# First block's merge: branch and output products as three float32r products of split halves, and two of three attention rounds for the large products

## The chip, the cores and the metric

The kernel runs on one core of one Trainium2 chip. The metric is the device time of one execution, in microseconds (us). TensorE (PE) multiplies, VectorE (DVE), ScalarE (ACT) and GpSimd (POOL) work on elements, SyncE (SP) issues the transfers from memory into a ring of five buffers in on-chip memory.

## What is computed

Two blocks on a sequence of 256 tokens with 1024 features, all in float32. The change is in the end of the first block. There two branches, `ya` (a gated delta rule) and `yb` (windowed attention with a sink, 8 heads of 64), are gated, projected, added and projected again:

```python
def _merge(ya, yb, ga, gb, w_proj_a, w_proj_b, w_out):
    y = jax.nn.sigmoid(ga) * (ya @ w_proj_a) + jax.nn.sigmoid(gb) * (yb @ w_proj_b)
    return y @ w_out

# in _layer: ga and gb are 1024-column slices of h @ w_in
ob = _latent_attention(qb, kb, vb, kb_c, vb_c, sink)
yb = ob * jax.nn.silu(zb)
x = x + gate[:, None] * _merge(ya, yb, ga, gb, w_proj_a, w_proj_b, w_out)
```

`ya`, `yb` are 256 x 512, `w_proj_a`, `w_proj_b` 512 x 1024, `w_out` 1024 x 1024. The second block (two layers, each with a feed-forward part, a mixer and a second feed-forward part) starts with a norm of the new `x` and takes the rest of the kernel.

## The kernel before

Every engine has a program of its own, written as a chain of Python functions. A step notes a name with `done(ins, name)`, a later step on any engine waits with `wait_ge(name)`. Each engine works strictly through its own list, so what stands ahead of a waiting instruction, and behind it, is set by the order in which the Python code is run. Where two or more things run beside each other on one engine, `run(...)` (L114) takes one step of each generator in turn: one such turn is called a round here. `slow(t, n)` (L125) gives a generator one step in every n rounds.

The stretch around the change has four parts.

1. **Attention** (`pe_attention` L1406, `act_attention` L1459, `v_attention` L1492). Four units u = 0 to 3, each 128 queries by 4 heads. For a unit PE makes four score products (into four PSUM banks), ACT copies their context half (L1473), DVE masks the other half (L1507), DVE takes the maximum (L1512) and some small steps (L1513 to L1515), ACT exponentiates (L1477, L1479), DVE finishes the denominator (L1517, L1518), PE transposes the probabilities (L384), ACT (L1485) and DVE (L1526) copy the transposes out, PE multiplies by the values (`ps<-arena ... 128x64`), DVE scales the result (L1530). The order on PE is: scores 0, scores 1, values 0, scores 2, values 1, scores 3, values 2, values 3; each is cut in halves of two heads. A unit's transposes wait for its softmax.
2. **Beside it** (`pe_beside` L1599 and its partners, slowed by n = 2): the last two column groups of `h @ w_in` (groups 5 and 6, the gate of branch b; on PE each is 16 products of 128x512, in four pieces of four), the norm and gate of `ya` (DVE L1631), its four transposes ("ya" turns), and the product with `w_proj_a` in four pieces of four matmuls (`ps<-ring,arena`), each multiplied into the gate by DVE (L1638). A third generator, `mods`, computes vector-matrix products for later gates, mostly on DVE (L522).
3. **Merge** (`pe_merge`, `act_merge`, `v_merge` L1642): DVE gates `yb` (L1645), PE transposes it (8 transposes), ACT copies the transposes out (L1561), PE multiplies by `w_proj_b` (16 matmuls of 128x512), DVE gates and adds (L1650, L1652, for each block of 128 tokens), PE transposes the sum (16), ACT copies (L1561), PE multiplies by `w_out` (32 matmuls of 128x512).
4. **Join**: DVE adds to `x` (L1734, L1740), ACT, DVE and POOL make the norm, PE transposes, and the first feed-forward part starts.

The matmuls of the merge are float32: each is written as two records in the trace. The feed-forward parts already work in another way: a float32 matrix is split into a high half, rounded to float32r (ACT L1913 for weights), and a low half, the difference (DVE L1962), and `mm3` (L386) makes three products, high x high, high x low, low x high, each one record.

SP's list holds, in this order, the loads of groups 5 and 6, of `w_proj_a` (2 MB in two buffers), `w_proj_b` (two), `w_out` (four) and the first feed-forward weights. A load waits until the buffer five loads earlier is released.

## Time and profile before

| | us |
|---|---|
| median of 3 runs | 1693.09 (1693.08 to 1705.6) |
| the profiled execution's own time | 1702.35 |
| its span, first to last instruction | 1700.6 |
| attention with what runs beside it, 307.8 to 414.6 | 106.8 |
| merge, 414.6 to 468.0 | 53.4 |
| all the rest | 1540.4 |

The profile is one execution. PE is busy for 92% of its span; busy does not mean full speed, since the profile also gives the clock that PE was granted (1.00 is 2.4 GHz, 0.50 is 1.2 GHz), and a matmul's record is longer than the distance to the next. DVE is busy for 60%, ACT 39%, POOL 14%.

### The profile page before, as it was taken

The numbers are of one execution on the slowest core, as the hardware profiler recorded it, in microseconds if no ns is written. First come the engines' busy times: TensorE is split into PE (matmuls) and PEld (weight loads), VectorE is DVE, ScalarE is ACT, GpSimd is POOL, SyncE is SP. The second block draws the span as 40 slices with busy tenths as digits, with TensorE's granted clock in tenths as the row PEclk, the third lists the DMA queues.
The fourth block names the chain that finished last, engine by engine and source line by source line (L and its number), as shares of the span: only waits on it lengthen the run. The fifth ranks groups of instructions, "written<-read, shape, count | busy, mean of one in ns | idle before, by whom it ended". The sixth has DMA issues, their size and how long they took to land.

```text
span 1700.6 us, 19133 instructions
## 1 busy us (share of the span) xinstructions
PE 1563.1 (92%) x7536; PEld 1154.5 (68%) x7536; DVE 1018.4 (60%) x1518; ACT 667.0 (39%) x1082; POOL 233.5 (14%) x243
## 2 busy tenths in 40 slices
PE   7997999888979989999979999799988999989998
PEld 1646566445468877775558877688877865477886
DVE  0477685741178887355348886478886453376654
ACT  2425221331155543361235552455532531155642
POOL 0231172000001100042001110011100241011100
PEclk9998999997989999999989998999999999989999
DMA  9434233531348879332347787378976322457551
GB/s 343 148 126 148 88 118 118 162 122 50 112 161 282 288 267 335 96 106 81 118 134 254 253 286 269 115 247 259 314 288 215 124 74 99 136 172 230 193 198 50
DMA packets 192096, 305.27 MB, mean 180 GB/s; under 512 B 6139, under 2 KB 116487, under 8 KB 191879
## 3 DMA queue, kind: packets, MB, share of 16 engines
q1 hardware_dynamic: 189088, 299.45, 52.3%
q10 hardware_dynamic: 2919, 4.61, 0.7%
q8 instruction: 59, 0.97, 0.2%
q14 instruction: 30, 0.25, 0.0%
HBM read 302.99 MB, written 1.05 MB: 179 GB/s over the span
## 4 chain that ended last, share of the span: by engine, by line
PE 69%; DVE 15%; ACT 7%; issue 3%; DMA 3%; POOL 2%; ACTq 0%; DVEq 0%; SPq 0%; POOLq 0%
PE ps L381 67%; DVE accs L522 3%; DVE wlo L1962 2%; DMA ring<-in_ffn_w_down_dram 2%; ACT whi L1913 2%; PE ps L384 1%; DVE H L1985 1%; DMA ring<-in_w_mod_dram 1%; ACT arena L1479 1%; DVE arena L1218 1%; DVE arena L1215 1%; DVE H L1800 1%; DVE misc L1512 1%; DVE H L1734 1%; ACT hh L1918 0%
## 5 line engine op out<-in xcount | busy, mean ns | idle before, releaser
L381 PE MATMUL ps<-hh,whi 128*128 128x512 f32 x1408 | 496.6, 404 | 27.1 <-DVE hh L1968 21.6
L1962 DVE TENSOR_TENSOR wlo<-ring,whi 128x1024 fp32r<-128x1024 f32 x264 | 323.8, 1231 | 180.9 <-ACT whi L1913 172.6
L1913 ACT ACTIVATE whi<-ring 128x1024 fp32r<-128x1024 f32 x264 | 273.4, 1054 | 280.1 <-PE ps L381 240.4
L381 PE MATMUL ps<-hh,wlo 128*128 128x256 f32 x1408 | 373.1, 286 | 0.0
L381 PEld LDWEIGHTS ps<-hh,whi 128*128 128x128 f32 x1408 | 259.2, 192 | 81.3 <-DVE hh L1968 22.4
L381 PE MATMUL ps<-ring,H 128*128 128x512 f32 (+1 forms) x608 | 268.7, 595 | 16.4 <-ACT arena L1013 9.0
L381 PEld LDWEIGHTS ps<-hh,wlo 128*128 128x128 f32 x1408 | 271.3, 193 | 17.1 <-issue 1.7
L381 PEld LDWEIGHTS ps<-ring,H 128*128 128x128 f32 x608 | 116.1, 197 | 141.9 <-issue 121.4
L522 DVE SCALAR_TENSOR_TENSOR accs<-ring,misc,accs 128x512 f32<-128x512 f32 x266 | 204.8, 770 | 2.6
L381 PE MATMUL ps<-H,ring 128*128 128x256 f32 (+1 forms) x576 | 157.5, 432 | 1.8 <-DVE H L1800 0.8
L381 PE MATMUL ps<-whi,ahi 128*128 128x512 f32 x352 | 143.2, 407 | 9.0 <-DVE H L1985 9.0
L381 PEld LDWEIGHTS ps<-arena 128*128 128x128 f32 (+3 forms) x1320 | 124.2, 171 | 33.5 <-issue 18.0
L381 PE MATMUL ps<-arena 128*128 128x64 f32 (+6 forms) x1320 | 136.8, 266 | 10.5 <-DVE arena L1526 6.8
L381 PEld LDWEIGHTS ps<-H,ring 128*128 128x128 f32 x576 | 109.8, 192 | 46.2 <-issue 30.6
L381 PE MATMUL ps<-wlo,ahi 128*128 128x512 f32 x352 | 139.9, 397 | 0.0
L381 PE MATMUL ps<-whi,alo 128*128 128x512 f32 x352 | 139.6, 397 | 0.0
L1951 POOL TENSOR_TENSOR alo<-H,ahi 128x256 fp32r<-128x256 f32 x88 | 66.7, 758 | 521.7 <-ACT ahi L1943 518.2
L381 PE MATMUL ps<-ring,arena 128*128 128x512 f32 x192 | 89.5, 623 | 3.3 <-ACT arena L2112 2.7
L381 PEld LDWEIGHTS ps<-whi,ahi 128*128 128x128 f32 x352 | 67.9, 193 | 25.3 <-DVE H L1985 10.3
L381 PEld LDWEIGHTS ps<-wlo,ahi 128*128 128x128 f32 x352 | 67.9, 193 | 14.9 <-issue 1.2
L381 PEld LDWEIGHTS ps<-whi,alo 128*128 128x128 f32 x352 | 67.8, 193 | 14.6
L1936 ACT ACTIVATE H<-ps 128x512 f32<-128x512 f32 x88 | 52.7, 599 | 58.0 <-PE ps L381 58.0
(290 smaller groups left out, 1410.5 us busy)
## 6 DMA issues: line engine op xcount, KB each, us to landing
ring<-in_w_mod_dram SPq DMA_DIRECT2D x84, 1024.0 KB, 7.3
ring<-in_w_in_dram SPq DMA_DIRECT2D x48, 1024.0 KB, 5.1
ring<-in_ffn_w_gate_dram SPq DMA_DIRECT2D x44, 1024.0 KB, 5.7
ring<-in_ffn_w_up_dram SPq DMA_DIRECT2D x44, 1024.0 KB, 5.7
ring<-in_ffn_w_down_dram SPq DMA_DIRECT2D x44, 1024.0 KB, 6.1
ring<-in_w_out_dram SPq DMA_DIRECT2D x12, 1024.0 KB, 4.8
gates<-in_b_mod_dram SPq DMA_DIRECT2D x7, 512.0 KB, 6.4
ring<-in_w_proj_a_dram SPq DMA_DIRECT2D x2, 1024.0 KB, 5.0
```

The costliest lines, as they stand in the source:

```text
L381: return self.e.matmul(o, lhsT, rhs, start=start, stop=stop)
L384: return self.e.transpose(o, in_, self.M.C["ident"])
L522: v.op(v.e.scalar_tensor_tensor(a, src, w, a, ALU.mult, ALU.add), *keys, *([("mod sum", c.n)] if kt == 7 else []))
L1215: v.op(v.e.tensor_tensor(t, M.AT[:, k, 0:k].unsqueeze(2).broadcast_to([128, k, w_]), M.XS[:, k, k:32].unsqueeze(1).broadcast_to([128, k, w ...
L1218: v.op(v.e.tensor_tensor(x, x, t, ALU.add))
L1479: a.done(a.e.activation(sm[:, t4, :], sm[:, t4, :], ACT.Exp, bias=nm[:, t4:t4 + 1], accum_out=den[:, t4:t4 + 1]), ("soft", u))
L1512: v.op(v.e.tensor_reduce(mx, sm, AX.X, ALU.max))
L1734: v.done(v.e.scalar_tensor_tensor(res[hf], two(M.ps((*ps, blk, hf))), factor, two(M.gates[:, gi, cols[hf]]), ALU.mult, ALU.mult), ("gated" ...
L1913: a.done(a.e.activation(hi, M.slot(key)[:, r0:r0 + rn, :], ACT.Copy), ("whi", l, sub, n))
L1936: a.done(a.e.activation(SG[x % 3], M.psum[:, b:b + 2, 256:512], ACT.Copy), ("copied", l, sub, x))
L1951: g.op(g.e.tensor_tensor(M.ALO[:, f, :], SG[f % 3][:, 0, :], plain(M.AHI[:, f, :]), ALU.subtract), ("alo", l, sub, f))
L1962: v.done(v.e.tensor_tensor(lo, M.slot(key)[:, r0:r0 + rn, :], plain(hi), ALU.subtract), ("split", l, sub, n), *([M.freed(key)] if ends els ...
```

## The change

The products with `w_proj_b` and `w_out` become three float32r products each, as in the feed-forward parts. The weights of `w_proj_b` are split into a high half by ACT, in the attention's last rounds (`act_beside`), and a low half by POOL, which is written back into the ring buffer (`ring_r` is the ring seen as float32r). For `w_out` ACT makes the high halves of the eight row groups (six once the attention is over, two after the second transposes), POOL the low halves of the first four, DVE of the other four. The transposed `yb` and sum are split too: ACT writes the high half where it wrote the copy before, DVE the low half. The products no longer wait for all transposes but for each one's low half. `slow` now gives the work beside the attention two steps in three rounds. ACT waits for the end of the `w_out` product before it writes the first feed-forward weights, because a high half lies there.

```diff
-def slow(t, n):
-    for _ in t:
-        for _ in range(n):
+def slow(t):
+    for i, _ in enumerate(t):
+        for _ in range(1 + i % 2):
             yield
...
+        self.HB = [self.WLO[:, 2, :], self.WLO[:, 3, :], alo[:, 2560:3584], alo[:, 3584:4608]]
+        self.HM = [k4(ahi, 0), k4(ahi, 1), self.WHI[:, 1, :], self.WLO[:, 0, :], k4(ahi, 2), k4(ahi, 3), self.WHI[:, 0, :], self.WHI[:, 3, :]]
...
 def pool_attention(g):
     pool_rstd(g, "o", 8)
+    for name in ("b", "m"):
+        for kt in range(4):
+            low_rows(g, name, kt)
...
+def pe_out(pe, name, lhs, nk):
+    M, (lhi, llo) = pe.M, lhs
...
+        key, _, hi, lo = merge_weights(M, name, kt)
+        pe.wait_ge(("rows split", name, kt), ("turned low", {"b": "yb", "m": "mt"}[name], kt))
+        c = slice(blk * 128, (blk + 1) * 128)
+        for hf in range(2):
+            s = slice(hf * 512, hf * 512 + 512)
+            ins = pe.mm3(bs[blk][hf], (lhi[:, kt, c], llo[:, kt, c]), (hi[:, s], lo[:, s]), kt == 0, kt == nk - 1)
...
-            ins = pe.mm(bs[blk][hf], lhs[:, kt, blk * 128:(blk + 1) * 128], M.slot(key)[:, kt % 2, hf * 512:hf * 512 + 512],
-                        kt == 0, kt == nk - 1)
...
+def act_high_rows(a, name, kt, *after):
+    key, w, hi, _ = merge_weights(a.M, name, kt)
+    a.wait_ge(key, *after)
+    a.done(a.e.activation(hi, w, ACT.Copy), ("rows high", name, kt))
...
+def low_rows(lane, name, kt):
+    _, w, hi, lo = merge_weights(lane.M, name, kt)
+    lane.wait_ge(("rows high", name, kt))
+    lane.done(lane.e.tensor_tensor(lo, w, plain(hi), ALU.subtract), ("rows split", name, kt))
...
+        v.done(v.e.tensor_tensor(lo[:, k, :], M.ps(key)[:, 0:256], plain(hi[:, k, :]), ALU.subtract), ("free", key), ("turned low", name, k))
...
 def act_beside(a):
...
     yield from act_turn(a, "ya", M.YAT, 2, 4, ("yat",))
+    for kt in range(4):
+        yield
+        act_high_rows(a, "b", kt)
...
 def act_merge(a):
     M = a.M
-    run(act_turn(a, "yb", M.YBT, 2, 4, ("ybt",)))
-    run(act_turn(a, "mt", M.MT, 2, 8, ("mt",)))
+    act_turn_high(a, "yb", M.YBH, 4)
+    for kt in range(6):
+        act_high_rows(a, "m", kt, ("o", "a", 1, 1), ("pv", 3, 3))
+    act_turn_high(a, "mt", M.MTH, 8)
+    for kt in (6, 7):
+        act_high_rows(a, "m", kt)
```

The order of instructions shows where the work beside the attention now stands. First PE, in the middle of the attention. In these rows `ring,H` is a piece of four products of column groups 5 and 6, `arena 128x512` are scores, `ctab,arena` are transposes (8 are half a unit's, 2 one "ya" turn), `arena 128x64` are products with the values, and `accs,ctab` belongs to `mods`. Before, from the second piece of group 6 to the values of unit 1:

```order
L381 MATMUL ps<-ring,H 128x512 x4
L381 MATMUL ps<-arena 128x512 x2
L381 MATMUL ps<-accs,ctab 128x512
L381 MATMUL ps<-arena 128x512 x2
L381 MATMUL ps<-ring,H 128x512 x4
L384 MATMUL ps<-ctab,arena 128x128 x8
L381 MATMUL ps<-ring,H 128x512 x4
L384 MATMUL ps<-ctab,arena 128x128 x8
L381 MATMUL ps<-arena 128x64 x8
```

and with the change, from the third piece of group 6 to the same values:

```order
L398 MATMUL ps<-ring,H 128x512 x4
L398 MATMUL ps<-arena 128x64 x8
L398 MATMUL ps<-ring,H 128x512 x4
L398 MATMUL ps<-arena 128x512 x2
L398 MATMUL ps<-accs,ctab 128x512
L398 MATMUL ps<-arena 128x512 x2
L401 MATMUL ps<-ctab,arena 128x128 x22
L398 MATMUL ps<-arena 128x64 x8
```

Both large pieces that stood behind the scores of unit 2 are ahead of them now; behind them stand 22 transposes alone (unit 1's 16 and three "ya" turns).

Second PE from the scores of unit 3 to the transposes of `yb` (the last 8). `ring,arena` is a piece of the product with `w_proj_a`. Before:

```order
L381 MATMUL ps<-arena 128x512 x2
L384 MATMUL ps<-ctab,arena 128x128 x20
L381 MATMUL ps<-arena 128x64 x16
L381 MATMUL ps<-ring,arena 128x512 x4
L384 MATMUL ps<-ctab,arena 128x128 x16
L381 MATMUL ps<-ring,arena 128x512 x4
L381 MATMUL ps<-arena 128x64 x16
L381 MATMUL ps<-ring,arena 128x512 x8
L384 MATMUL ps<-ctab,arena 128x128 x8
```

and with the change:

```order
L398 MATMUL ps<-ring,arena 128x512 x4
L398 MATMUL ps<-arena 128x512 x2
L398 MATMUL ps<-ring,arena 128x512 x4
L401 MATMUL ps<-ctab,arena 128x128 x8
L398 MATMUL ps<-ring,arena 128x512 x4
L401 MATMUL ps<-ctab,arena 128x128 x8
L398 MATMUL ps<-ring,arena 128x512 x4
L398 MATMUL ps<-arena 128x64 x16
L401 MATMUL ps<-ctab,arena 128x128 x16
L398 MATMUL ps<-arena 128x64 x16
L401 MATMUL ps<-ctab,arena 128x128 x8
```

The four pieces moved from behind unit 3's scores to among them and unit 2's transposes, and nothing large is left between the end of the attention and the transposes of `yb`.

Third ACT, from the scores of unit 3 to the last high half of `w_out`, with the change (`wlo<-ring`, `alo<-ring` up to the four copies of `yb`'s transposes, `wlo<-ps`, are the high halves of `w_proj_b`):

```order
L1493 ACTIVATE arena<-ps 128x256 x4
L1614 ACTIVATE wlo<-ring 128x1024
L1497 ACTIVATE misc<-misc 128x4
L1499 ACTIVATE arena,misc<-arena,misc 128x512 x4
L1505 ACTIVATE arena<-ps 128x512
L1614 ACTIVATE wlo<-ring 128x1024
L1505 ACTIVATE arena<-ps 128x512
L1614 ACTIVATE alo<-ring 128x1024 x2
L1505 ACTIVATE arena<-ps 128x512 x2
L1637 ACTIVATE wlo<-ps 128x256 x4
L1614 ACTIVATE ahi<-ring 128x1024 x2
L1614 ACTIVATE whi<-ring 128x1024
```

Before, the rows with `ring` were not there.

## Rows read from the trace of the kernel before

**Rows 1.** The page: engines, busy us, share of the span, instructions.
```profile
span 1700.6 us, 19133 instructions
PE 1563.1 (92%) x7536; PEld 1154.5 (68%) x7536; DVE 1018.4 (60%) x1518; ACT 667.0 (39%) x1082; POOL 233.5 (14%) x243
```

**Rows 2.** Stretches: length, busy us of each engine, PE clock, transfers.
```profile
core 0: us, PE busy (x) PEld busy (x) DVE busy (x) ACT busy (x) POOL busy (x), PEclk, DMA share, GB/s
372.10:414.60 42.50, 34.65 (x143) 22.61 (x143) 13.15 (x23) 8.90 (x21) 0.00 (x0) 0.84 0.07 25
```

**Rows 3.** PE in order of time, attention: start, us, what; idle before, its releaser.
```profile
331.81 1.91 PE L384 MATMUL ps<-ctab,arena 128*128 128x128 f32 x16
338.64 6.34 PE L381 MATMUL ps<-ring,H 128*128 128x512 f32 x8 [4.92 <-ACT arena L1013]
344.82 3.68 PE L381 MATMUL ps<-arena 128*128 128x64 f32 x32
...
356.79 3.70 PE L381 MATMUL ps<-ring,H 128*128 128x512 f32 x8
...
366.62 2.00 PE L381 MATMUL ps<-arena 128*128 128x64 f32 x16 [0.94 <-DVE arena L1526]
...
370.29 3.81 PE L381 MATMUL ps<-arena 128*128 128x64 f32 x20
...
376.30 2.40 PE L384 MATMUL ps<-ctab,arena 128*128 128x128 f32 x20
384.56 7.09 PE L381 MATMUL ps<-arena 128*128 128x64 f32 x32 [5.85 <-DVE arena L1526]
391.44 5.53 PE L381 MATMUL ps<-ring,arena 128*128 128x512 f32 x8
...
398.56 3.60 PE L381 MATMUL ps<-ring,arena 128*128 128x512 f32 x8
```

**Rows 4.** DVE in order of time: unit 3's maximum, the rest of its softmax.
```profile
377.36 2.29 DVE L1512 TENSOR_REDUCE misc<-arena 128x4 f32<-128x2048 f32 x1
...
383.40 0.16 DVE L1517 TENSOR_TENSOR misc<-misc 128x4 f32<-128x4 f32 x1 [3.16 <-ACT arena L1479]
```

**Rows 5.** PE in order of time, the merge.
```profile
414.60 1.06 PE L384 MATMUL ps<-ctab,arena 128*128 128x128 f32 x8 [2.01 <-DVE arena L1645]
416.31 17.07 PE L381 MATMUL ps<-ring,arena 128*128 128x512 f32 x32 [0.65 <-ACT arena L1561]
436.11 3.60 PE L384 MATMUL ps<-ctab,arena 128*128 128x128 f32 x16 [2.73 <-DVE arena L1652]
440.19 27.73 PE L381 MATMUL ps<-ring,H 128*128 128x512 f32 x64 [0.47 <-ACT H L1561]
```

**Rows 6.** PE in order of time, a feed-forward part's split products, 27 records.
```profile
655.05 0.39 PE L381 MATMUL ps<-whi,ahi 128*128 128x512 f32 x1
...
660.94 0.39 PE L381 MATMUL ps<-whi,alo 128*128 128x512 f32 x1
```

**Rows 7.** Groups of instructions: count, busy us, mean ns, idle before.
```profile
L381 PEld LDWEIGHTS ps<-wlo,ahi 128*128 128x128 f32 x34 | 6.4, 188 | 1.3
L1913 ACT ACTIVATE whi<-ring 128x1024 fp32r<-128x1024 f32 x264 | 273.4, 1054 | 280.1 <-PE ps L381 240.4 <-DMA ring<-in_ffn_w_down_dram 35.2 <-DMA ring<-in_ffn_w_up_dram 4.2
L2322 POOL TENSOR_TENSOR arena<-arena 128x1024 f32<-128x1024 f32 x12 | 25.2, 2102 | 68.8 <-DVE arena L2264 63.6 <-DVE arena L2277 4.9
L1951 POOL TENSOR_TENSOR alo<-H,ahi 128x256 fp32r<-128x256 f32 x88 | 66.7, 758 | 521.7 <-ACT ahi L1943 518.2
L1561 ACT ACTIVATE arena<-ps 128x256 f32<-128x256 f32 x8 | 2.7, 382 | 16.6 <-PE ps L384 16.6
L1990 DVE TENSOR_TENSOR H<-H 128x256 f32<-128x256 f32 x88 | 37.0, 422 | 7.2 <-ACT H L1939 1.8
L1740 DVE TENSOR_TENSOR X<-X,H 128x512 f32<-128x512 f32 x28 | 18.5, 683 | 0.0
L2274 DVE TENSOR_TENSOR arena<-arena 128x512 f32<-128x512 f32 x16 | 16.4, 1026 | 41.7 <-ACT arena L2223 23.7 <-PE ps L381 13.3 <-ACT arena L2224 4.2
```

**Rows 8.** ACT in order of time: the first feed-forward weights' high half.
```profile
476.67 1.06 ACT L1913 ACTIVATE whi<-ring 128x1024 fp32r<-128x1024 f32 x1
```

More of the change, by code:

```diff
@@ L205, in sb, with twice @@
         return self.ctx.enter_context(self.nc.sbuf_tensor(name, shape, f32))
+    def twice(self, name, shape):
+        with self.nc.sbuf_tensor(name, shape, f32) as plain_:
+            pass
+        return plain_, self.sbr(f"{name}_r", shape)
     def sbr(self, name, shape):
@@ L1562, in act_turn @@
         yield
+def pe_out(pe, name, lhs, nk):
+    M, (lhi, llo) = pe.M, lhs
+    bs = [[pe.bank(("o", name, blk, hf), "outx") for hf in range(2)] for blk in range(2)]
+    for blk, kt in [(b_, k_) for k_ in range(nk - 4) for b_ in range(2)] + [(b_, k_) for b_ in range(2) for k_ in range(nk - 4, nk)]:
+        key, _, hi, lo = merge_weights(M, name, kt)
[4 more added lines that the diff above has]
+            ins = pe.mm3(bs[blk][hf], (lhi[:, kt, c], llo[:, kt, c]), (hi[:, s], lo[:, s]), kt == 0, kt == nk - 1)
+        if kt == nk - 1 or (blk and kt % 2):
+            pe.done(ins, *([("o", name, blk)] if kt == nk - 1 else []), *([M.freed(key)] if blk else []))
 def sp_out(sp, name, w, nk):
@@ L1567, in sp_out, with merge_weights, v_turn, act_turn_high @@
         sp.full_rows(("out", name, k0), w, k0, 2)
-def pe_out(pe, name, lhs, nk):
-    M = pe.M
-    bs = [[pe.bank(("o", name, blk, hf), "outx") for hf in range(2)] for blk in range(2)]
-    for blk, kt in [(b_, k_) for k_ in range(nk - 4) for b_ in range(2)] + [(b_, k_) for b_ in range(2) for k_ in range(nk - 4, nk)]:
-        key = ("out", name, kt // 2 * 2)
-        pe.wait_ge(key)
-        for hf in range(2):
-            ins = pe.mm(bs[blk][hf], lhs[:, kt, blk * 128:(blk + 1) * 128], M.slot(key)[:, kt % 2, hf * 512:hf * 512 + 512],
-                        kt == 0, kt == nk - 1)
-        if kt == nk - 1 or (blk and kt % 2):
-            pe.done(ins, *([("o", name, blk)] if kt == nk - 1 else []), *([M.freed(key)] if blk else []))
+def merge_weights(M, name, kt):
+    key = ("out", name, kt // 2 * 2)
+    return key, M.slot(key)[:, kt % 2, :], (M.HB if name == "b" else M.HM)[kt], M.slot_r(key)[:, kt % 2, :]
+def act_high_rows(a, name, kt, *after):
[6 more added lines that the diff above has]
+    lane.done(lane.e.tensor_tensor(lo, w, plain(hi), ALU.subtract), ("rows split", name, kt))
+def v_turn(v, name, hi, lo, nk):
+    M = v.M
+    for k in range(nk):
+        key = ("turn", name, k)
+        v.wait_ge(("turned high", name, k))
+        v.done(v.e.tensor_tensor(lo[:, k, :], M.ps(key)[:, 0:256], plain(hi[:, k, :]), ALU.subtract), ("free", key), ("turned low", name, k))
+def act_turn_high(a, name, hi, nk):
+    M = a.M
+    for k in range(nk):
+        key = ("turn", name, k)
+        a.wait_ge(key)
+        a.done(a.e.activation(hi[:, k, :], M.ps(key)[:, 0:256], ACT.Copy), ("turned high", name, k))
 def sp_beside(sp):
@@ L1593, in sp_merge @@
     I = sp.M.I
-    run(slow(sp_beside(sp), 2), mods)
+    run(slow(sp_beside(sp)), mods)
     sp_out(sp, "b", I["w_proj_b"][0], 4)
@@ L1645, in v_merge @@
     v.done(v.e.tensor_tensor(M.OB, M.OB, M.ZB, ALU.mult), ("yb gated",))
+    v_turn(v, "yb", M.YBH, M.YBL, 4)
+    for kt in (4, 5):
+        low_rows(v, "m", kt)
     for blk in range(2):
@@ L2666, in tensor_program @@
     pe.sums = "row"
-    run(pe_attention(pe), slow(pe_beside(pe), 2), mods)
+    run(pe_attention(pe), slow(pe_beside(pe)), mods)
     pe.sums = "mods"
@@ L2688, in vector_program @@
     v.fence("delta")
-    run(v_attention(v), slow(v_beside(v), 2), mods)
+    run(v_attention(v), slow(v_beside(v)), mods)
     v_merge(v)
```

24 lines of the change are left out of this document (17 added, 7 removed).

## The prediction

> **What bounds the kernel now.** I read the page first: PE is busy for 92% of 1700.6 us [rows 1], so a change counts by what it does to PE's list, in matmul time, idle time and clock. Then the stretches: from the scores of unit 3 (372.1) to the transposes of `yb` (414.6) PE is busy for 34.65 of 42.5 us at a clock of 0.84 [rows 2]. Then PE in order of time, which shows where idle time and low clock lie. In the attention PE stands for 4.92 us until ACT has copied group 5 out (338.64), and for 5.85 us until DVE has copied unit 2's transposes (384.56). After each stop the clock is at its lower level: eight records of 128x512 take 6.34 and then 5.53 us, where they take 3.60 at the upper one, and 32 value records take 7.09 instead of 3.68 [rows 3]. So the first stop costs 4.92 + 2.7, the second 5.85 + 3.4 + 1.9. In the merge the reader sees a product of 17.07 us and one of 27.73 us, with only short stops around them [rows 5]: there matmul time is the price.
>
> **The two products.** A float32 matmul of 128x512 is two records; 64 take 27.73 us [rows 5], 0.867 us for a matmul. Three split products stand 0.2265 us apart (26 distances from 655.05 to 660.94 [rows 6]), 0.680 us. That saves 0.187 us each: 32 in the `w_out` product, **6.0 us** (27.7 to 21.8), and 16 in the `w_proj_b` product, **3.0 us**. The latter took 17.07 us, 3.2 more than 32 records at the upper clock (13.87); I keep these 3.2, since PE comes from the same kind of stop (2.01 us, eight transposes, 0.65 us).
> The Trainium skill (FP8 and Floating Point Precision, TensorE Precision Notes) says that true FP32 takes four passes through the array. With three single passes in their place a quarter would go, 3.5 and 6.9 us, 10.4 in all where the rows give 9.0; the rows' distance is 0.2265 us, and I go by it.
>
> **Starts of the products.** Before, the first matmul waited for all transposes to be copied, now only for its own row's high and low half. For `yb`: 1.71 us lay from the first transpose to the product (414.60 to 416.31 [rows 5]); now about 0.45 to the first transpose's end and its latency, 0.38 ACT, 0.42 DVE (the kind of [rows 7]): 1.3. For the sum: PE stands 0.47 us [rows 5] until the last copy, now nothing, as the first rows are split while PE transposes the others. **0.4 us** each.
>
> **The splits.** High halves: twelve on ACT at 1.054 us. Low halves: eight on POOL, four on DVE. The nearest rows for a POOL one are 2.10 us (128x1024, float32) and 758 ns for a quarter of it to float32r, so 3.03 at most [rows 7]; I take 2.1 to 3.0. ACT makes the first high half of `w_proj_b` before unit 3's softmax, the other three by 22 us after unit 3's scores begin; POOL is done with all at 28 to 31, and the product starts at 32.4. Hidden. For `w_out` ACT works from 33.0 to 39.3, POOL from 34 to 43 or 46, and the product starts at about 53. DVE's two (2.5 us) fall under the `w_proj_b` product, the last two of ACT and DVE under the first ten of sixteen pieces of the `w_out` product. Without that cover the first would cost ACT 1.05 + POOL 2.1 to 3.0. ACT's new wait ahead of the first feed-forward weights costs nothing: it came to them 8.7 us after the end of the `w_out` product (476.67 [rows 8] against 467.92 [rows 5]). Behind it stand only its own later splits. SP's list is the same; buffers come free earlier.
>
> **The attention.** PE has the same work, in another order.
> Up to 331.8 PE never stops, and the same ten pieces come first, so nothing changes. Then group 6 needs group 5 copied out; with that copy now ahead of unit 1's softmax on ACT, PE goes on at about 332.0: the stop of 4.92 and its 2.7 of low clock go. From there: first piece 3.6, transposes 1.9, piece 3.5, wait for DVE's copy 0.9 (its softmax 1 ends at 340.4), values 3.7, two pieces 7.2, scores and `mods` sum 4.9: the scores of unit 2 end at about 357.7. Before they ended at 356.79 with two pieces less done [rows 3].
> But these two pieces were what covered unit 2's softmax. From the end of the scores to the next values it takes 9.8 us (356.79 to 366.62 [rows 3]). PE now has 3.2 us of transposes for it, so **a new stop of some 6.4 us** opens, to 367.5. As the stops of 4.92 and 5.85 us lowered the clock and cost 2.7 and 5.3 us by that, I take 3.8 here. With 5.3 us of work (values 3.8, a "ya" turn, a sum) unit 3's scores begin at 376.6 instead of 372.1 (370.29 plus 16 of 20 records [rows 3]).
> From there on, t in us after that start: scores 1.9, piece 3.5, scores 1.9, piece 3.5, to 10.8. DVE multiplies that piece (0.7) before it takes the maximum, so the softmax starts at 11.5 and ends at 18.0 (2.29 + 0.65 + ACT 3.0 + 0.5; before 377.36 to 383.8 [rows 4]). PE in the meantime: transposes and pieces to 19.8, unit 2's values to 23.5, unit 3's transposes 25.4, values 29.2, then DVE's scaling and gating, 0.42 and 1.22 with gaps: transposes of `yb` at 31.1. Before that took 42.5 [rows 2]. The stop of 5.85 us and its low clock are gone here, and so are 8 us that the pieces took after it.
> Start of the transposes: 376.6 + 31.1 = 407.7 instead of 414.6, **6.9 us**. Bounds: if no clock loss belonged to short stops, before and after, the gain is 2.7 (403.9 against 406.6); if the new stop did not open, 10.6.
>
> **Sum.** 6.9 + 0.4 + 3.0 + 0.4 + 6.0 = 16.7 us. All behind the merge moves with it. The profiled execution's own time, 1702.35, would become 1685.7. It is 9.3 us above the median of the runs, 1693.09, so the median should be **1676.4 us**.
>
> **Rivals.**
> 1. The attention gains nothing (17 in 100). The new stop is as long as both old ones, or the clock stays low through the pieces behind it (7 us more for four at half speed). For it: the stop is 0.5 us longer than the longest before. Against it: unit 3 is shorter by 11.4. Only 9.8 us are left: 1683.3.
> 2. POOL and DVE hold each other up (12 in 100). For it: DVE's 128x512 with both inputs in `arena`, in a stage where POOL works too, takes 1026 ns where 683 is usual [rows 7]. A merge addition (L1652) or a split behind a POOL operation would wait 2.1 to 3.0 us; on the path is the second block's addition, and POOL should be done by then. Gain 13.7, time 1679.4. It turns into a PE wait if one POOL low half takes over 4.8 us (19 us for four).
> The Trainium skill (SBUF — State Buffer, Who interferes with whom) states that a DVE instruction with two SBUF inputs and a GpSimd instruction that reads SBUF shut each other out for the whole instruction. By it the DVE low halves of `w_out`, both inputs in SBUF, wait for POOL, while those of the transposes, one input from PSUM, do not.
> 3. The new stop hardly opens, as softmax 2 starts earlier than I work out (8 in 100): gain up to 20.4, 1672.7.
> 4. Slower (3 in 100): the weight load of a product is not hidden, when the moving half lies in the ring and the stationary one in `alo`. It takes 188 ns [rows 7] against a distance of 226; put end to end 414 ns, 144 times: 59.8 us instead of 32.6, a loss of 18 against float32's 41.6, and with the attention's 6.9 and the starts' 0.8 the kernel is 10 us slower, 1703.6. It decides from a distance of 0.343 us on (0.2265 + 16.7 / 144). The feed-forward rows speak against it.
> The forecast has 60 in 100.
>
> **Numbers.** A difference under 1% is about what a measurement of this kernel can't tell from none; 1% is 1676.2. The forecast's own range is 1672 to 1681, so it lies on both sides of the line: a little over half of its 60 and all of case 3 make 0.43 for faster; the rest of it and cases 1 and 2 make 0.53 for the same; 0.04 slower. The range takes in cases 1 to 3 and the bounds of the attention with the lower price of the products (2.7 + 9.0: 1681; 10.6 + 11.2: 1671) and some for runs whose clock falls otherwise: 1668 to 1687.
>
> **What would show it.** Right: `w_out`'s 96 records in about 22 us, `w_proj_b`'s 48 in 11 to 14.5; no stop for ACT L1030 at 332; one of 5 to 7 us ahead of unit 1's values; none of over 1.5 us from unit 3's scores to its end; PE in the merge released by DVE's low halves (L1629), never by POOL's (L1620). Wrong: a PE wait for L1620 (case 2), two stops of 5 us in the attention (case 1), split products over 0.25 us apart at the upper clock (case 4), or the gain given back in the feed-forward part behind.

## The result and the profile after

In paired runs the changed kernel takes 1680.96 us (median of six, 1680.03 to 1683.97), the kernel before 1699.13 us (median of six, 1693.08 to 1705.6). The ratio is 0.9895, with a 95% interval from 0.9875 to 0.9916: a gain of 1%, with the interval wholly below 1. A kernel counts as faster here only from 2% on, so the changed one is "the same", and so it is for every kernel below, down to the best ratio of 0.9828. The prediction drew the line at 1%, and its 0.43 for "faster" against 0.53 for "the same" was split at that line. The profiled execution took 1683.97 us (before 1702.35), its span is 1682.2 us (before 1700.6).

The page's head, as [rows 1] for before:
```profile
span 1682.2 us, 19265 instructions
PE 1550.8 (92%) x7584; PEld 1162.7 (69%) x7584; DVE 1031.2 (61%) x1534; ACT 678.1 (40%) x1094; POOL 254.3 (15%) x251
```
PE is busy for 12 us less; DVE, ACT and POOL have the splits on top.

PE of the changed kernel in order of time (start, us, what; idle before and its releaser), to compare with [rows 3] and [rows 5]:
```profile
341.83 2.01 PE L398 MATMUL ps<-arena 128*128 128x64 f32 x16 [1.01 <-DVE arena L1546]
343.67 5.35 PE L398 MATMUL ps<-ring,H 128*128 128x512 f32 x8
...
368.88 3.68 PE L398 MATMUL ps<-arena 128*128 128x64 f32 x16 [7.21 <-DVE arena L1546]
...
406.71 1.06 PE L401 MATMUL ps<-ctab,arena 128*128 128x128 f32 x8 [1.87 <-DVE arena L1704]
409.04 0.80 PE L398 MATMUL ps<-wlo 128*128 128x512 f32 x1 [1.27 <-DVE whi L1629]
409.64 0.63 PE L398 MATMUL ps<-ring_r,wlo 128*128 128x512 f32 x1
410.06 0.63 PE L398 MATMUL ps<-wlo,whi 128*128 128x512 f32 x1
...
413.02 0.40 PE L398 MATMUL ps<-wlo,whi 128*128 128x512 f32 x1
...
421.38 0.40 PE L398 MATMUL ps<-alo,whi 128*128 128x512 f32 x1
424.50 2.61 PE L401 MATMUL ps<-ctab,arena 128*128 128x128 f32 x16 [2.73 <-DVE arena L1714]
428.17 0.80 PE L398 MATMUL ps<-ahi,alo 128*128 128x512 f32 x1 [1.06 <-DVE alo L1629]
...
466.09 0.79 PE L398 MATMUL ps<-hh,whi 128*128 128x512 f32 x1 [5.11 <-DVE hh L2039]
```
The reader is to see four things: one stop of 7.21 us in place of two of 4.92 and 5.85; a product that begins behind a wait for DVE's low halves (L1629); matmuls 0.43 us apart at a product's start and 0.232 later; and the first feed-forward matmul at 466.09, where it was at 481.71. So 15.6 of the 18.4 us come from the code that was changed. The distance of 0.43 us for 512 columns belongs to the 1.2 GHz level, 0.232 to 2.4: from 429 to 433 us, where most of the matmuls stand 0.43 apart, the granted clock is 0.57, from 433 to 452, where they stand 0.232 apart, 1.00.

### The profile page after: what moved, and what is told of

It reads as the page before. It is cut to its first block, busy times and chain, and to the rows that moved or that the text cites. A ratio compares the mean times of both kernels' runs of the same rounds, so it can differ in the third digit from the quotient of the medians.

```text
span 1682.2 us, 19265 instructions
## 1 busy us (share of the span) xinstructions
PE 1550.8 (92%) x7584; PEld 1162.7 (69%) x7584; DVE 1031.2 (61%) x1534; ACT 678.1 (40%) x1094; POOL 254.3 (15%) x251
## 4 chain that ended last, share of the span: by engine, by line
PE 70%; DVE 14%; ACT 7%; issue 3%; DMA 3%; POOL 2%; ACTq 0%; DVEq 0%; SPq 0%; POOLq 0%
PE ps L398 69%; DVE accs L539 3%; DVE wlo L2033 2%; ACT whi L1982 1%; DMA ring<-in_ffn_w_down_dram 1%; PE ps L401 1%; DVE H L2056 1%; DMA ring<-in_w_mod_dram 1%; DVE arena L1235 1%; DVE arena L1232 1%; DVE H L1803 1%; DVE H L1869 0%; ACT hh L1987 0%; DMA ctab<-in_consts_dram 0%; ACT H L1878 0%
## 5 line engine op out<-in xcount | busy, mean ns | idle before, releaser
L2033 DVE TENSOR_TENSOR wlo<-ring,whi 128x1024 fp32r<-128x1024 f32 x264 | 323.5, 1230 | 178.0 <-ACT whi L1982 170.4
L398 PEld LDWEIGHTS ps<-hh,wlo 128*128 128x128 f32 x1408 | 271.2, 193 | 16.7 <-issue 1.4
L398 PE MATMUL ps<-ring,H 128*128 128x512 f32 (+1 forms) x544 | 239.8, 593 | 11.0 <-ACT arena L2183 5.6
L398 PEld LDWEIGHTS ps<-ring,H 128*128 128x128 f32 x544 | 103.8, 198 | 120.2 <-issue 104.9
L398 PE MATMUL ps<-whi,alo 128*128 128x512 f32 x376 | 148.4, 398 | 0.0
L398 PEld LDWEIGHTS ps<-whi,alo 128*128 128x128 f32 x376 | 72.5, 193 | 15.8
L398 PE MATMUL ps<-ring,arena 128*128 128x512 f32 x160 | 70.8, 595 | 2.6 <-ACT arena L2183 2.6
```

What stands on the lines that cost most here:

```text
L398: return self.e.matmul(o, lhsT, rhs, start=start, stop=stop)
L2033: v.done(v.e.tensor_tensor(lo, M.slot(key)[:, r0:r0 + rn, :], plain(hi), ALU.subtract), ("split", l, sub, n), *([M.freed(key)] if ends els ...
```

## Experiments: the two parts, each alone

**The order alone.** The kernel before with the new pattern of steps:
```
-def slow(t, n):
-    for _ in t:
-        for _ in range(n):
+def slow(t):
+    for i, _ in enumerate(t):
+        for _ in range(1 + i % 2):
             yield
```
(and the calls without the 2).

> The kernel before with one edit, the work beside the attention at two steps in three rounds; float32 products as before. Theory A (the order of the attention is worth its own 7 to 8 us, whatever the products are): 7 to 9 us faster than the kernel before, the transposes of yb near 406.7, a stop of about 7 us before unit 1's values, w_out's 64 records again in about 27.7 us. Rival B (the gain comes from the split products, and the order only moves a stop from one unit to another): within 2 us of the kernel before.

**The products alone.** The changed kernel with every second step again:
```
-        for _ in range(1 + i % 2):
+        for _ in range(2):
```


> The changed kernel with the work beside the attention back at every second round; the split products stay. Theory A: 7 to 10 us faster than the kernel before, 8 to 10 slower than the changed one, the transposes of yb near 414 to 416 and the stop of 5.85 us before unit 2's values back; the high halves of w_proj_b come partly after the attention now (ACT takes steps 14 to 17 of its list in rounds 27 to 33), so POOL's low halves of 2.35 us each may make PE wait 1 to 5 us at the w_proj_b product. Rival B: as fast as the changed kernel to 2 us.

Measured: the order alone 1687.78 us, ratio 0.9939 (0.9917 to 0.9961); the products alone 1685.45 us, ratio 0.9932 (0.9908 to 0.9955). PE with the order alone, and then with the products alone:
```profile
369.19 3.67 PE L381 MATMUL ps<-arena 128*128 128x64 f32 x16 [7.21 <-DVE arena L1526]
407.08 1.06 PE L384 MATMUL ps<-ctab,arena 128*128 128x128 f32 x8 [1.87 <-DVE arena L1645]
408.80 15.70 PE L381 MATMUL ps<-ring,arena 128*128 128x512 f32 x32 [0.65 <-ACT arena L1561]
427.22 1.94 PE L384 MATMUL ps<-ctab,arena 128*128 128x128 f32 x16 [2.73 <-DVE arena L1652]
430.03 27.73 PE L381 MATMUL ps<-ring,H 128*128 128x512 f32 x64 [0.88 <-ACT H L1561]
```
```profile
338.15 6.26 PE L398 MATMUL ps<-ring,H 128*128 128x512 f32 x8 [4.93 <-ACT arena L1030]
384.01 7.09 PE L398 MATMUL ps<-arena 128*128 128x64 f32 x32 [5.85 <-DVE arena L1546]
436.66 0.50 PE L398 MATMUL ps<-ahi,alo 128*128 128x512 f32 x1 [1.73 <-DVE alo L1629]
472.48 0.79 PE L398 MATMUL ps<-hh,whi 128*128 128x512 f32 x1 [5.05 <-DVE hh L2039]
```
The attention's gain belongs to the order: with it alone the `yb` transposes come at 407.08, 7.5 us earlier, and with the products alone both old stops are back. The `w_out` product took 27.73 us with the order alone; with the products alone it ran from 436.66 to 459.1, 22.4 us. The first feed-forward matmul comes 10.1 and 9.2 us earlier, with both parts 15.6: they don't add up, since the lower clock falls at other places in each (below).

For the order alone, theory A holds: transposes, stop and `w_out` product are as expected, and the time is 11.1 us under that of the kernel before (7 to 9 expected). For the products alone the rows are those of theory A, the old stops and the transposes at 414.00, but its times are not: 13.5 us faster than the kernel before, where 7 to 10 were expected, and 4.5 slower than the changed one, where 8 to 10 were. The trace has 6.4 us between the two up to the first feed-forward matmul. The wait for POOL did not come: PE waits 1.27 us at the `w_proj_b` product, for DVE (L1629), as in the changed kernel.

## Experiments: what stands before the products

**Other banks.** In the changed kernel the `yb` transposes use banks 7, 0, 1, 2 and the product behind them starts in bank 2. Its first matmul therefore waits for the last transpose's low half, though its own operands are there. The eight `mt` transposes end in bank 2 too.
```
+ "yb": (7, 6, 4, 5), "mt": (2, 3, 0, 1, 4, 5, 6, 7)}
-    run(pe_turn(pe, "yb", M.OB, 2, 4, "all", ("yb gated",)))
+    run(pe_turn(pe, "yb", M.OB, 2, 4, "yb", ("yb gated",)))
-    run(pe_turn(pe, "mt", M.GA, 2, 8, "all", ("merged",)))
+    run(pe_turn(pe, "mt", M.GA, 2, 8, "mt", ("merged",)))
```


> The changed kernel with other PSUM banks for the transposes of yb (7, 6, 4, 5) and of the sum (2, 3, 0, 1 first). In the changed kernel the first bank of each product (2) is the one that the last transpose holds, so PE waits 1.27 and 1.06 us until DVE has made all low halves. Theory A (it is the bank, not the first row's low half): the two stops shrink to 0.3 us and nothing, 1 to 2 us faster than the changed kernel. Rival B (the stop is ACT's and DVE's latency for the first row): stops and time unchanged. Rival C: stops shrink, but the clock is at its lower level for as long, so that less than 1 us is gained.

Measured: 1676.49 us, ratio 0.9862 (0.9837 to 0.9887). PE:
```profile
407.53 1.06 PE L401 MATMUL ps<-ctab,arena 128*128 128x128 f32 x8 [1.87 <-DVE arena L1704]
408.96 0.47 PE L398 MATMUL ps<-wlo 128*128 128x512 f32 x1 [0.37 <-DVE whi L1629]
425.32 2.51 PE L401 MATMUL ps<-ctab,arena 128*128 128x128 f32 x16 [3.42 <-DVE arena L1714]
427.86 0.76 PE L398 MATMUL ps<-ahi,alo 128*128 128x512 f32 x1
```
The bank was the cause: 1.43 us from the start of the transposes to the product instead of 2.33, and 2.54 instead of 3.67. But 0.7 us of it goes back at once, in a stop of 3.42 instead of 2.73 before the `mt` transposes. That is DVE, late for the gating, as the next experiments show. From the `yb` transposes to the first feed-forward matmul the path is 1.7 us shorter (57.67 us instead of 59.38). The runs can't tell that much: the intervals of both kernels overlap.

**POOL works longer.** Rows 4 and 5 of `w_out` are split by POOL, behind its other eight, instead of DVE:
```
-    for name in ("b", "m"):
-        for kt in range(4):
+    for name, nk in (("b", 4), ("m", 6)):
+        for kt in range(nk):
             low_rows(g, name, kt)
```


> The changed kernel with the low halves of w_out's rows 4 and 5 taken from DVE and given to POOL, behind its other eight. Nothing is left out. Theory (POOL and DVE hold each other up when both read SBUF, and it costs nothing in the changed kernel only because the last addition of the gating, 1.22 us, falls just behind POOL's end): POOL now works on until about 426 us, that addition takes 2.1 to 2.7 us, the mt transposes begin 0.9 to 1.5 us later (at 425.4 to 426.0 in place of 424.50) and the time grows by that, 0.1%. Rival (there is no such contention, DVE's 2.7 us had another cause): the addition stays at 1.22, the transposes at 424.5, and the time is the same.

Measured: 1679.61 us, ratio 0.9898 (0.9874 to 0.9922), the same as the changed kernel within the interval, which is wider than what was to be seen. The trace decides. DVE and POOL of the changed kernel first, then DVE, POOL and PE of this one:
```profile
413.12 5.43 DVE L1620 TENSOR_TENSOR ring_r<-ring,ahi 128x1024 fp32r<-128x1024 f32 x2 [4.13 <-ACT ahi L1614]
418.47 1.27 DVE L1712 TENSOR_TENSOR arena<-arena,ps 128x512 f32<-128x512 f32 x2
419.78 2.12 DVE L1714 TENSOR_TENSOR arena<-arena 128x1024 f32<-128x1024 f32 x1
423.13 1.22 DVE L1714 TENSOR_TENSOR arena<-arena 128x1024 f32<-128x1024 f32 x1
...
417.43 3.38 POOL L1620 TENSOR_TENSOR ring_r<-ring,wlo 128x1024 fp32r<-128x1024 f32 x1
```
```profile
423.87 2.40 DVE L1712 TENSOR_TENSOR arena<-arena 128x1024 f32<-128x1024 f32 x1
...
417.13 2.44 POOL L1620 TENSOR_TENSOR ring_r<-ring,wlo 128x1024 fp32r<-128x1024 f32 x1
419.48 5.70 POOL L1620 TENSOR_TENSOR ring_r<-ring,ahi 128x1024 fp32r<-128x1024 f32 x2
...
426.41 3.60 PE L401 MATMUL ps<-ctab,arena 128*128 128x128 f32 x16 [3.90 <-DVE arena L1712]
```
The last addition, 1.22 us when POOL has finished, takes 2.40 beside it, and PE's stop is 3.90 instead of 2.73. (The path up to the first feed-forward matmul is no longer for it, 59.29 us from the `yb` transposes instead of 59.38: in this execution the `w_out` product ran at the upper clock from its start.) DVE's low halves of the rows take 2.7 us each beside POOL, as against 1.23 (1230 ns, the mean of 264 such subtractions in the feed-forward parts), and POOL's 3.38 us instead of 2.4. So rival 2's mechanism is in the changed kernel; it costs nothing there, but only just. DVE is busy without a pause from 413.12 to 421.90, and the product that it waits for ends at about 421.8; the next operation of DVE, which needs that product, begins at 421.82. The Trainium skill (SBUF — State Buffer, Who interferes with whom) says that a DVE instruction with two SBUF inputs and a GpSimd instruction that reads SBUF exclude each other; the rows agree. L1712 has one input from PSUM and was not stretched: two take 1.27 us at 418.47, beside POOL's subtraction, and 1.28 us with the order alone, where POOL does nothing then.

## Experiments: the low clock

**Idle work in the merge's stops.** PE multiplies a piece of the identity, into a bank that is written anew later, while it would stand:
```
+def fill(pe, b, n):
+    if b in pe.held:
+        pe.wait_ge(("free", pe.held[b]))
+    for _ in range(n):
+        pe.mm(pe.M.psum[:, b, 0:64], pe.M.C["ident"], pe.M.C["ident"][:, 0:64])
+    fill(pe, 4, 15)
     run(pe_turn(pe, "yb", M.OB, 2, 4, "all", ("yb gated",)))
+    fill(pe, 4, 10)
     pe_out(pe, "b", (M.YBH, M.YBL), 4)
...
```
and the like, 22 ahead of the `mt` transposes and 8 ahead of the `w_out` product.

> The changed kernel with idle work on PE in its four stops of the merge: 15, 10, 22 and 8 small products (128x64, of the identity, into a bank that is written anew later) ahead of the yb transposes, w_proj_b's product, the mt transposes and w_out's product. Nothing of the reference is left out. Theory (the low clock in the two products follows the stops): no distance of 0.43 us is left between the products' matmuls, w_proj_b's product takes 48 x 0.2325 = 11.2 us in place of 12.57 and w_out's 96 x 0.2325 = 22.3 in place of 24.53, the stops being no longer than they were; the first ffn matmul comes at 466.1 - 3.6 = 462.5 us, and the time is some 3.6 us under the changed kernel's (about 1677). Rival (the low clock has nothing to do with stops of 1 to 3 us, or the idle products run over into the transposes and take back what they give): the products keep 12.6 and 24.5 us, or a stop grows by what they save, and the first ffn matmul stays at 466 to 467.5.

The same with 7, 5, 11 and 4:

> The changed kernel with idle work on PE in the four stops of the merge again, at half the length (7, 5, 11 and 4 small products, 0.234 us each by the run with the long fill, so 1.6, 1.2, 2.6 and 0.9 us), so that it ends about when the stop does. Nothing is left out. Theory (the products ran slow at their start because PE had stood; the long fill cured it and lost the gain by running 1.1 to 2.3 us past each stop): the granted clock is 1.00 from 404 to 453 us, the stops end where they ended in the changed kernel, and the first ffn matmul comes 1.4 + 2.2 us before 466.09, at 462.5; median about 1677. Rival (short fills leave the clock low as the stops did): the products take 12.6 and 24.5 us and the first ffn matmul stays at 466.

Measured: the long fill 1677.15 us, ratio 0.9887 (0.9856 to 0.9917); the short one 1680.02 us, ratio 0.9899 (0.9884 to 0.9915). Stretches (length, busy us of each engine, granted clock) of the changed kernel, then with the long fill:
```profile
409.00:422.00 13.00, 12.74 (x48) 9.95 (x48) 8.85 (x6) 5.03 (x6) 11.43 (x4) 0.89 0.13 40
422.00:428.00 6.00, 2.61 (x16) 2.23 (x16) 4.96 (x11) 3.00 (x9) 0.00 (x0) 0.80 0.75 266
428.00:453.00 25.00, 24.52 (x96) 19.46 (x96) 5.24 (x8) 2.76 (x6) 0.00 (x0) 0.91 0.35 104
```
```profile
409.00:422.00 13.00, 13.00 (x67) 10.89 (x66) 8.83 (x9) 6.11 (x8) 11.48 (x4) 1.00 0.12 27
422.00:428.00 6.00, 6.00 (x55) 5.96 (x55) 3.67 (x5) 0.65 (x3) 0.00 (x0) 1.00 0.80 294
428.00:453.00 25.00, 25.00 (x120) 20.36 (x118) 7.35 (x14) 4.89 (x13) 0.00 (x0) 1.00 0.32 102
```
Without stops the clock is 1.00 throughout, and the two products take 11.2 and 22.3 us instead of 12.6 and 24.5. The long fill ran past the stops and took the gain back: the first feed-forward matmul came at 467.10, not at the 462.5 of the expectation. The median of 1677.15 that the expectation had named is not that gain, then; it came out by luck, in the rest of the program (1209.0 us in this profile, 1216.1 in the changed kernel's). The short one didn't, yet from the attention's last values (401.16 in the changed kernel, 396.15 here) to the first feed-forward matmul (466.09, 459.72) it needs 63.57 us instead of 64.93: 1.4 us gained, not the 3.6 of my expectation. (All of this execution lies 5 us earlier, since its clock was higher in code that is the same in both.) PE with the short fill:
```profile
415.24 2.56 PE L398 MATMUL ps<-ctab 128*128 128x64 f32 x22
419.47 1.94 PE L401 MATMUL ps<-ctab,arena 128*128 128x128 f32 x16 [1.67 <-DVE arena L1722]
423.13 0.50 PE L398 MATMUL ps<-ahi,alo 128*128 128x512 f32 x1 [0.88 <-DVE alo L1637]
```
From the product's end (415.24) to the `mt` transposes there are now 4.23 us instead of 2.89. The product ends 1.4 us earlier, DVE does not (5.42 us for its two low halves beside POOL): the margin is gone, and rival 2's price, 1.3 us, stands on the path. Another 0.6 us went in the join, where the lower clock fell on the first transposes (0.57 in their first microsecond instead of 0.92) and ACT got them 3.7 us after they began instead of 3.1.

**DVE's two low halves moved**, from ahead of the gating to behind the low halves of the `mt` transposes, in the kernel that has the other banks and the placement of the steps that is shown below:
```
-    for kt in (4, 5):
-        low_rows(v, "m", kt)
     ...
     v_turn(v, "mt", M.MTH, M.MTL, 8)
-    for kt in (6, 7):
+    for kt in (4, 5, 6, 7):
```


> Banks and placement as before, with DVE's low halves of w_out's rows 4 and 5 moved from ahead of the gating to behind the low halves of the mt transposes. Nothing is left out. Theory (once the product begins earlier, DVE is late to the gating since its low half beside POOL's takes 3.41 us, so rival 2's cost has come onto the path): the stop ahead of the mt transposes shrinks from 4.08 to about 2.7 us, w_out's product finds its rows 4 and 5 ready some 10 us after its start as before, and the first ffn matmul comes about 1.3 us earlier, near 460 us. Rival (the gating was bound by something else, or w_out's product now waits for row 4): the stop stays near 4 us, or a new stop stands in w_out's product and the first ffn matmul stays at 461.2 or later.

Measured: 1670.66 us, ratio 0.9843 (0.9827 to 0.9859). The stop before the transposes is 2.73 us where it was 4.08 with banks and placement together (first measured below), and no new one stands in the `w_out` product. The first half of the expectation holds; the second doesn't: the first feed-forward matmul came at 461.17, as before the move (461.20). The lower clock had fallen on the start of the `w_out` product (23.2 us instead of 22.3) and on the transposes of the join (13.9 us from the product's end to the first feed-forward matmul instead of 12.9).

## Experiments: another placement in the attention

The large products are placed by a table of steps, so that two of them stand beside unit 2's softmax:
```
+PE_AT = [1, 2, 4, 5, 7, 8, 13, 15, 18, 19, 20, 20, 21, 22, 23, 25]
-    run(pe_attention(pe), slow(pe_beside(pe)), mods)
+    run(pe_attention(pe), placed(pe_beside(pe), PE_AT), mods)
```
(and the like for DVE and ACT).

> The changed kernel with the steps beside the attention placed by a list of rounds: group 6's last two pieces behind unit 2's scores, three pieces of the w_proj_a product behind unit 3's, one ahead of unit 3's transposes. Theory A (the attention is bound by the softmax chain of 9.8 us per unit only where PE has no large piece to put behind the scores): the stop of 7.21 us before unit 1's values falls to under 1.5 us, its low clock (2.6 us) goes too, no stop over 1.5 us opens elsewhere, 6 to 9 us faster than the changed kernel. Rival B (the chain on DVE and ACT is as long as PE's work, so a stop only moves): a stop of 4 us or more opens at unit 2's or unit 3's values, less than 3 us faster.

Together with the other banks:

> The two single changes together that were each better than the changed kernel: other banks for the yb and mt transposes, and the large products placed at other steps of the attention. Nothing is left out. Theory (they work at different places, so they add up): yb transposes at 405.5, w_proj_b's product 1.4 us behind them, w_out's product without a stop, first ffn matmul at about 463.5, median 1667 to 1670. Rival (what the second gained was the low clock falling elsewhere by chance): the first ffn matmul is at 463.5 all the same, but the rest of the program takes 1210 to 1218 us in place of 1206 and the median is 1672 to 1677.

The latter with idle work ahead of the two rows of transposes and of the `w_proj_b` product:

> The kernel before this one (banks and placement) with idle work on PE ahead of the yb transposes (15 small products), of w_proj_b's product (3) and of the mt transposes (26). Nothing is left out. Theory (low clock follows the stops): both products run at 0.2325 us apart from their first matmul on, 11.2 and 22.3 us, the first ffn matmul comes 3 us earlier than without the fill (about 460.5), median some 3 us lower. Rival: no change of the products' times, first ffn matmul within 0.5 us of the kernel without the fill.

Measured: placement alone 1671.42 us, ratio 0.9841 (0.9817 to 0.9865); with the banks 1677.46, 0.9874 (0.9847 to 0.9901); with the fill 1679.91, 0.9902 (0.9879 to 0.9925). PE of the first:
```profile
345.01 7.39 PE L408 MATMUL ps<-arena 128*128 128x64 f32 x20 [0.52 <-DVE arena L1556]
...
358.05 5.37 PE L408 MATMUL ps<-ring,H 128*128 128x512 f32 x8
...
405.45 1.60 PE L411 MATMUL ps<-ctab,arena 128*128 128x128 f32 x8 [1.87 <-DVE arena L1714]
```
The stop of 7.21 us is gone, but the transposes come only 1.3 us earlier: behind two stops of 1.03 and 0.52 us PE ran at the lower clock from 345 to 361 us (20 records of 128x64 in 7.39 us, which take 3.8 at the upper level). The first feed-forward matmul comes at 464.39, 1.7 us earlier. The stop of 4 us or more that rival B expected elsewhere did not open, but its gain of less than 3 us is what the rows show. The runs show more: all four took 1669.53 to 1673.65 us, and the changed kernel's six 1680.03 to 1683.97. Of the 11.8 us between the two profiles 10.1 lie behind the first feed-forward matmul, in instructions that are the same. So theory A's 6 to 9 us came out in the time, but not from the attention; whether the placement has a part in them is not shown.

Banks and placement together bring the first feed-forward matmul to 461.20, the earliest until then, and the whole kernel is no faster for it. Here the expected median failed, and its rival, in the rest of the program, is what was seen (1214.4 us instead of 1206.0, median 1677.46). The fill, again at the long size, ran past the stops: the `w_proj_b` product began at 408.78 instead of 406.31, and the first feed-forward matmul came at 464.90.

**Does filling take the low clock away, or only move it?** In the kernel with rows 4 and 5 late: idle work in unit 0's stops, and ahead of both rows of transposes; then in unit 1's stops and ahead of the `w_proj_a` product too, of which this is the last form:
```
+            if u < 2 and t4 % 2 == 0:
+                for _ in range(4 - t4):
+                    pe.mm(bo[:, 256:320], M.C["ident"], M.C["ident"][:, 0:64])
...
+            if u == 1 and t4 == 1:
+                for _ in range(3):
...
+            for _ in range(0 if blk or hf else 2):
...
```


> The kernel with rows 4 and 5 late, with idle work on PE in the stop ahead of unit 0's values (4 small products), in the one inside them (2), ahead of the yb transposes (7) and of the mt transposes (11). Nothing is left out. Theory (the 17 us at the lower clock from 344 to 361 us come from the stops of 1.0 and 0.5 us there): PE runs at the upper clock there, which gives 8 us: yb transposes at 397 to 398 in place of 404.9, both products at 0.2325 us a matmul, first ffn matmul at 449 to 450, and the whole 6 to 10 us faster than the kernel without the fill. Rival (that stretch is not due to the short stops but to what PE did before, or is only put off): the lower clock stands there all the same or falls on later work, yb transposes at 403 or later, and the whole is within 3 us of the kernel without the fill.

> The kernel with rows 4 and 5 late and idle work in unit 0's stops, with idle work in the stops of unit 1 and ahead of w_proj_a's product too (4, 3, 2 and 2 small products), where the lower clock began in the run before (364 to 385 us, behind stops of 0.95, 0.73 and 0.52 us). Nothing is left out. Theory (the lower clock needs a stop of some tenths of a microsecond ahead of it, wherever it falls): with no stop over 0.4 us left between 340 and 404 us, the granted clock is 1.00 there, yb transposes come at 398 to 399 in place of 407.7, the first ffn matmul at 452 to 453, and the time is some 5 us under that of the kernel without this fill. Rival (the chip lowers the clock after so much work at the upper one, stops or not, so that filling only moves it): the low stretch stands there without a stop ahead of it, or comes later, yb transposes at 405 to 408 or the products slow, and the first ffn matmul stays at 460 to 462.

Measured: 1667.26 us, ratio 0.9833 (0.9809 to 0.9857), and 1668.42 us, ratio 0.9828 (0.9808 to 0.9848). Stretches of both:
```profile
340.00:362.00 22.00, 20.80 (x103) 13.05 (x101) 15.26 (x27) 7.92 (x18) 0.00 (x0) 1.00 0.34 123
362.00:404.00 42.00, 40.74 (x154) 24.03 (x153) 12.61 (x23) 14.24 (x28) 9.34 (x4) 0.76 0.20 78
```
```profile
304.00:441.00 137.00, 131.44 (x604) 87.20 (x603) 71.15 (x124) 50.42 (x106) 21.59 (x10) 1.00 0.40 143
441.00:470.00 29.00, 22.11 (x112) 19.74 (x113) 18.54 (x30) 16.70 (x28) 1.35 (x2) 0.82 0.43 143
```
With unit 0 filled, the low stretch moved behind the next stops (0.95, 0.73 and 0.52 us); with those filled too it went. From 309 us to the end of the `w_out` product at 439 the longest stop is now 0.60 us. (Ahead of 309 stands one of 1.60 us, which has the upper clock behind it in every kernel here.) So the first expectation failed and its rival, that the low clock falls on later work, held: `yb` transposes at 407.68, first feed-forward matmul at 461.30. The second held in the trace: transposes at 398.70, and the first feed-forward matmul at 453.32, 12.8 us before the changed kernel's. It failed in the time, which is not 5 us lower but 1.2 higher. Against the kernel without any fill (0.9843) neither gain is clear of the intervals.

In the stretches filled here the lower clock came behind stops of 0.5 to 1 us and went with them. But a stop is not enough. The kernel with the short fill has the same instructions as the changed one up to 399 us, and there the stop of 1.02 us had the upper clock behind it, eight records in 3.65 us where the changed kernel took 5.35:
```profile
337.86 2.00 PE L398 MATMUL ps<-arena 128*128 128x64 f32 x16 [1.02 <-DVE arena L1546]
339.69 3.65 PE L398 MATMUL ps<-ring,H 128*128 128x512 f32 x8
```
In the kernel before, stops of 0.94 and 0.51 us after 365 us left the clock at 1.00 (360 to 376 us), and with the products alone the `w_out` product ran at 1.00 from its start, behind a stop of 1.73 us. What decides whether the clock falls after a stop, no experiment here shows.

The Trainium skill (TensorE: Matmul & The Clock Gate, A second HAM failure mode) tells of a kernel whose short idles between groups of matmuls made the clock change to and fro; the rows with the placement alone, with stops of 1.03 and 0.52 us and 16 us at the lower level behind them, are of that kind.

## The rest of the program

From the first feed-forward matmul on, every kernel here has the same instructions. The stretch from there to the end, in order: before, the changed kernel, placement alone, rows 4 and 5 late, all filled:
```profile
481.71:1700.60 1218.89, 1139.38 (x5596) 906.32 (x5596) 768.40 (x1025) 531.20 (x791) 145.92 (x148) 0.97 0.58 196
466.09:1682.20 1216.11, 1140.69 (x5596) 908.36 (x5596) 768.28 (x1025) 531.21 (x791) 145.91 (x148) 0.97 0.58 196
464.39:1670.40 1206.01, 1128.51 (x5596) 898.50 (x5596) 768.37 (x1025) 531.70 (x791) 146.18 (x148) 0.98 0.59 198
461.17:1668.90 1207.73, 1131.30 (x5596) 901.08 (x5596) 768.14 (x1025) 531.31 (x791) 146.10 (x148) 0.97 0.58 197
453.32:1671.40 1218.08, 1141.52 (x5596) 908.08 (x5596) 768.29 (x1025) 532.29 (x791) 145.99 (x148) 0.97 0.57 196
```
PE has 5596 matmuls in each, and its busy time differs by 13.0 us from least to most (1128.51 to 1141.52); the length of the stretch differs by nearly the same (1206.01 to 1218.89). DVE and ACT differ by less than 1.1 us. So it is PE's clock that differs. (In all fourteen profiled executions the stretch takes 1206.0 to 1219.1 us, with no clear order by how early it begins, though the two that begin earliest, at 453.32 and 459.72, have 1218.1 and 1219.1.) Much of this changes from one execution to the next of the same kernel: twelve executions of the kernel before took from 1692.85 us at a mean granted clock of 0.965 to 1705.45 at 0.955. But it is not shown to be chance alone: the four runs with the placement alone lie within 4.1 us of each other, and so do the four with the short fill, some 9 us higher.

So the last kernel's 8 us over the one with unit 0 filled (453.32 against 461.30) did not reach its end: 0.9828 and 0.9833 are the same. In the profiled executions its rest was 4.4 us longer (1218.08 against 1213.70), and each of the two was the slowest execution of its kernel (1673.17 of 1665.94 to 1673.17 us, 1676.81 of 1663.57 to 1676.81). Whether the chip gives such a gain back regularly, or the executions fell badly, stays open; the intervals are some 3 us wide to each side.

## Why the prediction was right, and where it was not

From profile to profile, up to the first feed-forward matmul:

| step | predicted | measured |
|---|---|---|
| attention, up to the `yb` transposes | 6.9 | 7.9 |
| `yb` transposes to product | +0.4 | -0.6 |
| `w_proj_b` product | 3.0 | 4.5 |
| gating, up to the `mt` transposes | 0 | -0.2 |
| `mt` transposes to product | +0.4 | +0.4 |
| `w_out` product | 6.0 | 3.2 |
| join | 0 | 0.4 |
| sum | 16.7 | 15.6 |
| rest of the program | 0 | 2.8 |

That the sum is off by only 1.1 us is in part luck: its terms are off by up to 2.8 us, and the errors of the attention and of the `w_proj_b` product (2.5 together) cancel most of that of the `w_out` product.

**The attention** went as worked out. Unit 3's scores began at 376.35 (376.6 forecast) and the transposes came 30.4 us later (31.1). The new stop was 7.21 us, not 6.4, and the clock behind it cost 2.6, not 3.8. A loss not foreseen stands at 343.67: eight records in 5.35 us behind a stop of only 1.01. Rivals 1 and 3 are out by this. Neither was priced well: four pieces at half the clock would cost some 14 us, not 7, since one takes 3.6 [rows 3], and without the new stop of 6.4 and its 3.8 the attention's gain would be 17.1, not 10.6.

**The splits** were hidden, as worked out: POOL was done with the low halves of `w_proj_b` at 402.6, 6.4 us before the product, and with its four of `w_out` at 420.8, 7.4 us before.

**"Now only for its own row's high and low half"** failed for `yb`: the step looked at the operands and not at where the product writes. The banks experiment shows it. For `mt` the same wait exists (1.06 us), but the transposes ran in 2.61 us instead of 3.60, so the 0.4 came out by luck, by another cause.

**The `w_out` product, 6.0 us,** was mis-sized: 3.2. Its matmuls stand 0.2325 us apart at the upper clock, not 0.2265 as in the feed-forward rows (0.6 us), and for its first 4.3 us they stand 0.43 apart, which costs 2.2 us with what follows at the change of level. With the products alone this product took 22.4 us, and with the fills 22.3: the split itself is worth 5.4 us. The forecast took a clock loss into account behind the long stops and, for `w_proj_b`, kept the old one (it was smaller, hence 4.5); for `w_out` it had none.

**Rival 2** named a real mechanism and the right rows; what kept it off the path was 0.1 us at most, not the 4.8 us per low half of the forecast, which asked only when PE would wait for POOL itself. PE never did. What mattered was when DVE comes free for the gating. **Rival 4** is out: at the upper clock the split products stand 0.2325 us apart, where it needed 0.343. Of the signs, two of those for "right" were missed, `w_out`'s records in about 22 us (24.5) and the stop of 5 to 7 us (7.21); none of those for "wrong" came.

**From profile to median.** The forecast for the profiled execution was 1685.7 us; it took 1683.97. The median was put 9.3 us below, as 1693.09 was below 1702.35; but over six runs the median of before was 1699.13, only 3.2 below. That step, not the sum, put 1676.4 where 1680.96 was measured.

## What to carry to other kernels

When an operand's wait is loosened, look at the destination as well: a product that starts in the bank of the last transpose waits for all of them. Ask of a helper engine that overlaps another not only who waits for it, but when the engine that it slows comes free; a margin of 0.1 us or less is gone with the next improvement. And where PE's clock has two levels, judge an edit by the time from a common point to the end of the changed code, with the clock of each step beside it, and the kernel by many runs: 13 us between two executions of the same instructions is more than most edits are worth.

## What the hardware did that was not expected

- Stops of 0.5 to 1.0 us could be followed by the lower clock, at a cost of 1.7 us (at 343.67 in the changed kernel) up to some 8 us (345 to 361 with the placement). The stop of 7.21 us in the changed kernel cost 2.6.
- They need not be: the same stop of 1.0 us, behind the same instructions, had the lower clock after it in the changed kernel and the upper one with the short fill; in the kernel before, stops of 0.94 and 0.51 us had the upper one.
- With all filled, 130 us (309 to 439) with no stop over 0.60 us ran at a granted clock of 1.00.
- POOL's 128x1024 subtraction from float32 to float32r took about 2.4 us alone and 3.38 beside DVE's, which took 2.7 instead of 1.23.
- Split products whose operands lie in the ring and the arena's weights stand 0.2325 us apart in the changed kernel, those of the feed-forward parts 0.2265 [rows 6]; the cause was not looked for.
